# Hybrid attention layer on eight cores: order of the first loads, third projection without shift, kv block of group B ahead of attention A

## The reference

```python
sh1, sc1, ga1, sh2, sc2, ga2 = split(silu(cond) @ w_mod + b_mod, 6)   # cond per request
h = rms_norm(x, g_attn_pre) * (1 + sc1) + sh1
qA, kA, vA, qB, kB, vB = split(h @ w_in)          # w_in: 2048 x 4608
oA = neighbourhood_attention(qA, kA, vA, cache_a_k, cache_a_v, rpb)   # latent: 8 x 16 window plus bias
oB = attend(rope(rms_norm(qB)), [cache_b_k, rope(rms_norm(kB))], [cache_b_v, vB])
x = x + ga1 * rms_norm(concat(oA, oB) @ w_out)
x = x + ga2 * rms_norm(conv_ffn(rms_norm(x) * (1 + sc2) + sh2))
```

## Time and profile before

| what | us |
|---|---|
| median of 3 runs | 3124.49 (3123.12 to 3428.13) |
| the profiled execution, its time | 3145.39 |
| its span on the slowest core (core 2) | 3143.8 |
| spans of its eight cores | 3110.4 to 3143.8 |
| TensorE busy in the span | 2931.7 (93%) |

### The profile page before, as it was taken

The page is one execution under the profiler, slowest core; times in us unless marked ns, Lnnn a source line. Parts: engine busy times, 40 slices in busy tenths (PEclk is TensorE's granted clock), DMA queues, the critical chain, the costliest instruction groups (busy, mean ns, idle before and its releaser), DMA issues.

```text
span 3143.8 us, 39804 instructions; the slowest of 8 cores (3110.4 to 3143.8 us)
## 1 busy us (share of the span) xinstructions
PE 2931.7 (93%) x15020; PEld 1375.2 (44%) x15020; DVE 1304.8 (42%) x1822; ACT 1026.7 (33%) x1787; POOL 157.5 (5%) x263
## 2 busy tenths in 40 slices
PE   0689899989999999999998998989999999999997
PEld 0335433444444444444444444544444444444443
DVE  0326734655540443443444345245540343442445
ACT  1236766444322220220225145644322220220223
POOL 0003500000000000000000000000000000000001
PEclk9999999999999999999998899999999999999999
DMA  9879545594636446438446675383625424435438
GB/s 180 173 128 152 85 78 98 98 195 134 114 66 113 76 72 114 71 64 142 70 83 165 117 153 102 84 170 140 136 54 97 82 51 91 81 62 96 78 64 117
DMA packets 40305, 333.62 MB, mean 106 GB/s; under 512 B 4726, under 2 KB 7846, under 8 KB 15542
## 3 DMA queue, kind: packets, MB, share of 16 engines
q0 software_dynamic: 23472, 263.48, 49.1%
q1 hardware_dynamic: 16646, 67.60, 6.4%
HBM read 533.68 MB, written 44.07 MB: 184 GB/s over the span
## 4 chain that ended last, share of the span: by engine, by line
PE 86%; DMA 5%; ACT 3%; DVE 2%; issue 2%; another core or an unknown queue 1%; POOL 0%; SPq 0%; DVEq 0%; ACTq 0%; POOLq 0%
PE PS L1433 84%; PE PS L1434 2%; ACT M L1435 2%; DMA M<-xs 1%; DMA M<-modrows 1%; ACT M L1436 1%; DMA M<-w_mod 1%; DMA M<-w_in 1%; DMA sbk<-M 1%; DMA M<-xp 0%; DVE M L1441 0%; DVE M L1440 0%; DVE M L1438 0%; ACT stats L1435 0%
## 5 line engine op out<-in xcount | busy, mean ns | idle before, releaser
L1433 PE MATMUL PS<-M 128*128 128x512 bf16 (+2 forms) x12960 | 2812.3, 375 | 37.2 <-ACT M L1435 18.0
L1433 PEld LDWEIGHTS PS<-M 128*128 128x128 bf16 x12960 | 1246.6, 99 | 1508.0 <-issue 197.9
L1441 DVE SCALAR_TENSOR_TENSOR M<-PS,taps,M 128x1023 f32<-128x1023 f32 (+1 forms) x352 | 451.0, 1281 | 784.2 <-ACT M L1435 765.5
L1435 ACT ACTIVATE M<-PS,taps 128x1024 f32<-128x1024 f32 x176 | 211.5, 1203 | 929.5 <-PE PS L1433 929.5
L1435 ACT ACTIVATE M<-M 128x1024 f32<-128x1024 f32 (+5 forms) x268 | 235.7, 879 | 475.4 <-DVE M L1441 297.5
L1439 DVE TENSOR_TENSOR M<-PS,M 128x512 f32<-128x512 f32 (+2 forms) x320 | 204.5, 661 | 401.5 <-PE PS L1433 276.2
L1436 ACT COPY M<-PS 128x512 f32<-128x512 f32 (+5 forms) x309 | 201.7, 664 | 391.0 <-PE PS L1433 302.0
L1434 PE MATMUL PS<-identb,M 128*128 128x128 bf16 x1300 | 114.9, 234 | 114.2 <-DVE M L1440 81.6
L1434 PEld LDWEIGHTS PS<-identb,M 128*128 128x128 bf16 x1300 | 94.1, 105 | 157.0 <-issue 136.0
L1440 DVE TENSOR_SCALAR M<-M,stats 128x256 bf16<-128x256 bf16 (+4 forms) x164 | 89.1, 561 | 157.7 <-ACT stats L1435 143.6
L1435 ACT ACTIVATE M<-PS,negB 128x512 bf16<-128x512 f32 x192 | 128.0, 686 | 44.9 <-PE PS L1433 42.0
(11 more groups left out here) (65 smaller groups left out, 559.6 us busy)
## 6 DMA issues: line engine op xcount, KB each, us to landing
M<-w_up POOLq DMA_DIRECT2D x40, 2048.0 KB, 15.8
M<-w_mod POOLq DMA_DIRECT2D x24, 2048.0 KB, 20.3
M<-w_down POOLq DMA_DIRECT2D x32, 1408.0 KB, 12.1
M<-w_in POOLq DMA_DIRECT2D x18, 2048.0 KB, 17.3
M<-xs SPq DMA_DIRECT2D x16, 1024.0 KB, 17.2
M<-w_out POOLq DMA_DIRECT2D x8, 2048.0 KB, 23.4
M<-xp SPq DMA_DIRECT2D x16, 1024.0 KB, 7.1
ys<-M SPq DMA_DIRECT2D x8, 1024.0 KB, 5.9
```

What stands on the lines that cost most here:

```text
L1433: "matmul": lambda e, kw: e.matmul(**kw),
L1435: "activation": lambda e, kw: e.activation(**kw),
L1441: "scalar_tensor_tensor": lambda e, kw: e.scalar_tensor_tensor(**kw),
```

## The change

1. All eight tiles of latent rows get buffers of their own (`X0`) and their loads are issued right after `cond`; `mrows` goes between the second and the third, and `gq_bc` and `gk_bc` now stand behind all eight on SP's queue. The first weight load waits until the tile with index 5 has landed.
2. The list `FIRST` is reordered: vA0 is loaded right after kA0, ahead of the four `c0` blocks. kvB no longer needs the token, which is gone; `tables` is queued for tick 6.
3. vA0 runs on the scaled, unshifted rows `hS` too: tiles 6 and 7 are copied to SBUF, six tiles stay in PSUM banks 0 to 5. `mod_col(0, 0)` and `(0, 1)` stand between its tiles. The shift's share is a row: 16 matmuls of the broadcast shift `shB` with the weights, added by `fix_v` to each tile. kA0 runs without a `mod_col` in it.
4. `modulate` now gives DVE tokens 0 to 639 and ACT 640 to 1023.
5. kvB of the first group runs alone, before the cached keys and the mask are handled and before attention A starts; attention A is woven into qB0 and qB1 alone, with shares 0.45 and 0.75. The four blocks of `w_mod` that were in kvB and qB0 move on by one projection.

```diff
-                dma("pool", mb(e[3], e[2][0] * e[2][1]), e[1], "w%d" % int(e[3]))
+                dma("pool", mb(e[3], e[2][0] * e[2][1]), e[1], "w%d" % int(e[3]), rk=[("xin", 5)] if i == 0 else ())
...
-        MODS = {"qA0": [], "kA0": [], "vA0": [], "kvB": [(2, 0), (2, 1), (2, 2)], "qB0": [(2, 3)], "qB1": [(3, 0)],
-                "kA1": [(3, 1), (3, 2)], "vA1": [(3, 3), (4, 0), (4, 1)], "qA1": [(4, 2), (4, 3)]}
+        MODS = {"qA0": [], "kA0": [], "vA0": [], "kvB": [], "qB0": [(2, 0), (2, 1)], "qB1": [(2, 2), (2, 3)],
+                "kA1": [(3, 0), (3, 1)], "vA1": [(3, 2), (3, 3), (4, 0)], "qA1": [(4, 1), (4, 2), (4, 3)]}
-        FIRST = [("c", 1, 0, s0), ("qA0", s1), ("c", 1, 1, s2), ("c", 1, 2, WX_AT), ("c", 1, 3, E_AT), ("kA0", s0), ("c", 0, 0, s2), ("c", 0, 1, WX_AT),
-                 ("c", 0, 2, E_AT), ("c", 0, 3, s2), ("vA0", WX_AT), ("kvB", s2), (2, 0), (2, 1), ("qB0", s0), (2, 2), ("qB1", s2), (2, 3),
-                 ("kA1", s0), (3, 0), ("vA1", s2), (3, 1), (3, 2), ("qA1", s0), (3, 3), (4, 0), (4, 1), (4, 2), (4, 3)]
+        FIRST = [("c", 1, 0, s0), ("qA0", s1), ("c", 1, 1, s2), ("c", 1, 2, WX_AT), ("c", 1, 3, E_AT), ("kA0", s0), ("vA0", s2), ("c", 0, 0, WX_AT),
+                 ("c", 0, 1, E_AT), ("c", 0, 2, WX_AT), ("c", 0, 3, E_AT), ("kvB", WX_AT), ("qB0", s0), (2, 0), ("qB1", s2), (2, 1), (2, 2),
+                 ("kA1", s0), (2, 3), (3, 0), (3, 1), ("vA1", s2), (3, 2), (3, 3), ("qA1", s0), (4, 0), (4, 1), (4, 2), (4, 3)]
-                        add_in(g, e[0], e[1], ("S",) if e[0] == "kvB" else ())
+                        add_in(g, e[0], e[1])
...
+        X0 = (32, 40, 48, 56, 144, 152, 172, 180)
+        for t in range(NT):
+            dma("sp", mf(X0[t], 2048), xg[GROUPS[0]][t * 128:(t + 1) * 128, :], "x%d" % t, wk=[("xin", t)])
+            if t == 1:
+                dma("sp", cst[0:48, :], mrows, "ca")
+        dma("pool", maskb[:], mask_d, "c6")
+        w_pump()
         for i, (g_d, g_t) in enumerate(((g_qn, gq_bc), (g_kn, gk_bc))):
             dma("sp", g_t[:], bass.AP(g_d, 0, [[0, 128], [1, 128]]), "c%d" % (2 + i))
...
-            if i in (1, 4):
-                mod_col(0, i // 3, 6, 7)
+        Wv = w_get("in%dvA0" % g)
+        vf = {6: mf(188, 512), 7: mf(190, 512)}
+        vbank = {6: 0, 7: 1, 0: 2, 1: 3, 2: 4, 3: 5, 4: 0, 5: 1}
+        for n, t in enumerate((6, 7, 0, 1, 2, 3, 4, 5)):
+            for c in range(16):
+                mm(bank(vbank[t]), hS[:, c, t * 128:(t + 1) * 128], Wv[:, c, :], c == 0, c == 15)
+            if t > 5:
+                op("act", "copy", out=vf[t], in_=bank(vbank[t]))
+            if n in (1, 5):
+                mod_col(0, n // 4, 6, 7)
         mod_col(0, 2, 6, 7)
         mod_col(0, 3, 6, 7)
+        shB = mb(40, 2048).rearrange("p (c m) -> p c m", c=16)
+        vrow = mf(44, 512)
+        op("dve", "tensor_copy", out=shB, in_=modcols[:, 1, g, :].unsqueeze(2).to_broadcast([128, 16, 128]))
...
+        for c in range(16):
+            mm(bank(6), shB[:, c, :], Wv[:, c, :], c == 0, c == 15)
+        w_done("in%dvA0" % g)
-        modulate(g, 0, 0, 512)
-        modulate(g, 0, 512, 1024, "act")
+        modulate(g, 0, 0, 640)
+        modulate(g, 0, 640, 1024, "act")
+        op("act", "copy", out=vrow, in_=bank(6))
...
+        def fix_v(ts):
+            for t in ts:
+                op("dve", "tensor_tensor", out=vv[:, 2 + t, :, :].rearrange("p h d -> p (h d)"), in0=vf[t] if t > 5 else bank(vbank[t]), in1=vrow, op=ALU.add)
+        fix_v((4, 5, 0, 1, 2, 3))
+        later(3, fix(*fixes[0]))
+        later(4, lambda _: fix_v((6, 7)))
+        later(5, fix(*fixes[1]))
...
-            mark("S")
-        later(4, tables)
+        later(6, tables)
...
+                run_all(dense_in(g, "kvB", (6, 7), (0, 1)))
+                flush((0, 1))
+...
-            for k, nm in enumerate(("kvB", "qB0", "qB1")):
-                corun(dense_in(g, nm, (6, 7), None, mods[nm]), 28.5, sA, (0.28, 0.38, 0.6)[k])
+            for k, nm in enumerate(("qB0", "qB1") if first else ("kvB", "qB0", "qB1")):
+                corun(dense_in(g, nm, (6, 7), None, mods[nm]), 28.5, sA, ((0.45, 0.75) if first else (0.28, 0.38, 0.6))[k])
```

More of the change, by code:

```diff
@@ L402, in build_program @@
                     elif isinstance(e[0], str):
-                        add_in(g, e[0], e[1], ("S",) if e[0] == "kvB" else ())
+                        add_in(g, e[0], e[1])
                     else:
-                        add_mod(*e, WX_AT if e == (2, 1) else s1)
+                        add_mod(*e, s1)
                 homes = (s2, s1, s0, WX_AT)
@@ L423, in build_program @@
                         add_mod(5, M5[qd, j])
-        dma("pool", maskb[:], mask_d, "c6")
-        w_pump()
+        X0 = (32, 40, 48, 56, 144, 152, 172, 180)
+        cst = mf(198, 128)
         dma("sp", identf[:], ident_d, "c0")
@@ L438, in build_program @@
             op("pe", "transpose", out=PS[:, r * 16:(r + 1) * 16], in_=stg0[0:16, r, :], identity=identf[0:16, 0:16])
-        condT = mf(192, 32)
+        condT = mf(191, 32)
         op("dve", "tensor_copy", out=condT, in_=PS[:, 0:32])
@@ L541, in modulate, with norm1 @@
                     op("act", "activation", out=h, in_=h, func=AF.Identity, scale=sc, bias=sh)
-        def norm1(g, x_ats, xn_ats, tb):
+        def norm1(g, x_ats, xn_ats, tb, ahead=True):
             def load(t):
@@ L548, in norm1 @@
             nx = len(x_ats)
-            for t in range(nx - 1):
+            for t in range(nx - 1 if ahead else 0):
                 load(t)
             for t in range(NT + 2):
-                if t + nx - 1 < NT:
+                if ahead and t + nx - 1 < NT:
                     load(t + nx - 1)
@@ L1034, in build_program @@
         g = GROUPS[0]
-        cst = mf(198, 128)
-        dma("sp", cst[0:48, :], mrows, "ca")
         cols = mf(198.5, 48)
@@ L1043, in build_program @@
         qf = [mf(172 + 4 * h, 1024) for h in range(4)]
-        kf = [mf(at, 1024) for at in (160, 164, 144, 148)]
+        kf = [mf(at, 1024) for at in (156, 160, 144, 148)]
         mcnt = [0]
@@ L1049, in by_groups @@
             mcnt[0] += 1
-            part = mf(188 + 2 * (mcnt[0] % 2), 512)
+            part = mf(192 + 2 * (mcnt[0] % 2), 512)
             for cc in range(4):
@@ L1078, in mod_col @@
                 op("dve", "tensor_tensor", out=dst, in0=dst, in1=bc, op=ALU.add)
-        n1 = Side(norm1(g, (144, 152, 172, 180), (160, 164, 168), [(4, 5), (2, 3)]), 10.0)
+        n1 = Side(norm1(g, X0, (160, 164, 168), [(4, 5), (2, 3)], False), 10.0)
         n1.finish()
@@ L1115, in build_program @@
         for k, nm in enumerate(("kA0", "qA0")):
-            fixes.append((nm, 2 + k) + by_groups(shT, w_get("in%d%s" % (g, nm)), 2 + k))
+            part, rest = by_groups(shT, w_get("in%d%s" % (g, nm)), 6 + k)
+            op("dve", "tensor_copy", out=part, in_=bank(6 + k))
+            fixes.append((nm, rest))
             w_done("in%d%s" % (g, nm))
-        modulate(g, 0, 0, 512)
-        modulate(g, 0, 512, 1024, "act")
+        for c in range(16):
[4 more added lines that the diff above has]
+        op("act", "copy", out=vrow, in_=bank(6))
         def fix(nm, rest):
@@ L1133, in fix @@
             return go
[L1135 to L1138, removed]
+        def fix_v(ts):
[5 more added lines that the diff above has]
+        later(5, fix(*fixes[1]))
+        tst = mf(196, 512).rearrange("p (j q) -> p j q", j=4)
         dma("sp", tst[0:88, 0:3, :], conv_w.rearrange("j (c p) -> c j p", p=128), "c4")
@@ L1158, in build_program @@
                 mod_begin(2, 140, 0)
+                run_all(dense_in(g, "kvB", (6, 7), (0, 1)))
+                flush((0, 1))
+                for j in range(4):
+                    op("pe", "transpose", out=PS[:, 512 + j * 88:512 + (j + 1) * 88], in_=tst[0:88, j, :], identity=identf[0:88, 0:88])
+                op("dve", "tensor_copy", out=taps[:, :, :], in_=PS[:, 512:512 + 352].rearrange("p (j c) -> p j c", j=4))
+                for fn in go_on:
+                    fn()
+                bias_mask()
             else:
                 sF = Side(final(GROUPS[0], G2, f_tiles(), fss), 10.0)
[L1161 to L1176, removed]
+            for k, nm in enumerate(() if first else ("qA0", "kA0", "vA0")):
+                corun(dense_in(g, nm, (4, 5, 6, 7), (0, 1), mods[nm]), 28.5, sF, 1.0 / (3 - k))
             while not first and sF.t < 10.0:
```

## The result

The changed kernel takes 3173.33 us (median of 4, 3171.95 to 3175.95) against 3124.48; the ratio is 1.0159, 95% interval 1.0139 to 1.0179. It is 49 us slower; 3141 was forecast, with a range to 3163.

The account below looks back on a forecast made before the run. TensorE, busy 93% of the span, was taken as the bound outside the start. Attention A ending 15 us later, norm1's 5 us gain included, plus a moved block made +16 on 3124.5, rounded to 3141 us; range 3113 to 3163.

Parts of the forecast that it names:

- Part 1: Start, x rows first: norm1 still waits for gq_bc and gk_bc behind x on SP's queue; gain 5 us.
- the bound of 14: Norm1 at the start: upper limit of the gain, 14 us, if each queued load takes 12.2 us.
- The rule of whole packets: DMA queues at the start: round robin by packets would land both gains near 45 us, giving 3118; chance 0.15.
- Part 2: Weight order from qA0 to kvB: kvB's weights land behind c0_3, so kvB starts at 228.5 instead of 233.3 us.
- Part 3: Loads behind kvB: cached keys and bias table queue behind three blocks; first bias at 281.1, about 21 us idle.
- main case: Whole kernel: bias table landing late holds attention A; 3141 us, own range 3131 to 3152, chance 0.60.
- rival B: Before attention A: tables not behind the weights, start near 263 once kvB is flushed; 3123 us, chance 0.08.
- Part 4: Attention A in two projections: weaving no worse, stretch of 128.9 us ending at 410.0, 15 us later than 395.
- sign of being wrong: Attention A: the prediction is wrong if the two projections woven with it take over 60 us each.
- Rival C: Attention A packed too densely: TensorE waits for the exponent every unit, 20 us more; 3161 us, chance 0.12.
- The blocks behind: Stages behind attention A: order kept, weights have over 20 us for a 15.2 us load; moved block adds 1.0.
- runs tell nothing apart within 2%: Whole kernel: no change within 2% (62 us) can be told; same 0.97, faster 0.01, slower 0.02.

Follow-up runs that it names:

- f_part1: Kernel before with only eight x buffers, x rows loaded ahead of the weights and the two gains behind x: 3102.21 us, ratio 0.9935.
- d_token: Changed kernel with the load of qB0 waiting for tables, so cached keys and bias table precede it in the queue: 3174.5 us against 3173.
- c_shares: Changed kernel with attention A's shares in qB0 and qB1 at 0.28 and 0.38 instead of 0.45 and 0.75: 3141.85 us, ratio 1.0063.
- b_kv_woven: Changed kernel with kvB woven into attention A again (shares 0.28, 0.38, 0.6) and qB0's load waiting for tables: 3136.09 us, ratio 1.0043.
- j_mods: Changed kernel with two blocks of w_mod in qA1 instead of three, and three in kA1: 3159.01 us, ratio 1.0117.
- k_cols_early: Changed kernel with the four shift blocks used earlier, two between the tiles of kA0 and two between those of vA0: 3162.75 us, ratio 1.0127.
- e_gains_woven: Changed kernel with the loads of gq_bc and gk_bc ahead of x and kvB woven into attention A again: 3116.77 us, ratio 0.9971.
- m_best_woven: Changed kernel with gains ahead of x, kvB woven into attention A, shift blocks used early and two w_mod blocks in qA1: 3115.85 us, ratio 0.9978.
- h_gains_shares: Changed kernel with the loads of gq_bc and gk_bc ahead of x and shares 0.28 and 0.38: 3119.96 us, ratio 0.9998.
- n_best_alone: Changed kernel with gains ahead of x, shift blocks early, two w_mod blocks in qA1, kvB alone, shares 0.28 and 0.38: 3112.65 us, ratio 0.9969.

## Why the prediction was wrong

**Part 1.** The mechanism held: SP's queue served in order, norm1 behind `gq_bc` and `gk_bc`. The size was off: three turns beside weights were counted, for tile 7 and the two gains, and two came. All of x had been moved by about 30 us (8.5 MB on SP's queue), before the weights took their share, so tile 7 cost no turn; the gains were seen at 45.8 and 59.3, 13.5 us apart instead of 15.5. The gain was 20 us, not 5, and outside the bound of 14. The experiments show it a real gain (f_part1), which the rest gave back. The rule of whole packets in the Trainium skill ("DMA: Bandwidth & Descriptors", "Queues, rings and completion order"), by which, as the prediction worked it out, both gains would land close behind each other, does not fit 45.8 and 59.3.

**Part 2.** The wait for `c0_3` came as worked out (5.9 us), and kvB started at 221.5 instead of 228.5. Against the kernel before, norm1's 20 us were 15 after the stages of qA0, which took 41.3 us instead of 36.6 at a lower granted clock (0.50 to 0.83 in most windows of 10 us between 70 and 120), and 12 at kvB. That the queue stood still for 30 us was in the forecast's own numbers, `c0_2` only after 183, but was not named as a cost.

**Part 3.** The time was right, 281.1 against 279.0 (276.3 by the mean over the cores), but in part by luck, as another wait held it. d_token shows that the loads did not decide: with `rpbt` there 16 us earlier the bias is first added at the same time. What ended last was kvB's flush and, behind it, the chain of the cached keys. The main case had no flush after kvB's matmuls; only rival B had one, at 263.

**Part 4 is the step that failed.** "It fits, tightly" compared busy sums: 44 and 45 us of VectorE and ScalarE beside 54 of TensorE. The stretch was put at 128.9 us and measured 162 (279 to 441). The busy sums were right: qB0 had 41 us of VectorE and 42 of ScalarE, qB1 47 and 45. That they would then run beside TensorE at full rate was wrong: two projections took 79 and 65 us, 144 instead of 108, over the 60 that the prediction had named as a sign of being wrong. The wait that it had left out is TensorE's for the exponent, 2.1 to 2.6 us in about every second unit of qB0's first half and 24 us in all, against 7 in c_shares; most of the rest is matmuls at the lower clock. Rival C had the place and the kind of wait right (TensorE on the exponent), but priced it from the drain at 0.7 us a unit, 20 us in all; its price had to hold the convoy, in which the exponent stands behind a copy that itself waits for TensorE, and the lower clock seen after most of these stops. c_shares takes 31 us back by the shares alone, and its stretch is 129.1 us by the mean over the cores: the time forecast for the weaving is there once attention A is woven in no denser than before. b_kv_woven takes 37 back.

**The blocks behind.** "Over 20 us for a load of 15.2" was worked out for halves. qA1 got three blocks; one was used at 616.0 and the next was wanted 12 us later, so its load was 3.9 us late (632.21 above). The stretch up to the end of qA1 cost 7 us instead of 1, and j_mods takes 6 of them back.

The sum: 15 was forecast for kA1's start. The two traced cores give 46, but the one of before asks for the second cached keys as the first of its eight, at 393.9, and the one of the change as the last, at 438.3; by the means over the cores it is 37 (396.3 and 433.0). That is the 15, less 5 for a first bias ahead of its forecast, and 28 for part 4. For the blocks 1 was forecast and 7 came. Together 44 against the 49 measured on the slowest cores; the other 5 are within what cores differ. By steps between kernels: part 1 -20 (3102), parts 2 to 4 of the change with the new blocks +34 (3136), kvB alone with the higher shares +37 (3173). The prediction's remark that runs tell nothing apart within 2% does not hold for these: the interval of the result is 0.2% to either side.

What stays open is how much of the +34 belongs to vA0 without shift as such: k_cols_early and j_mods give 11 and at least 6 on the changed kernel, but together only 1 on e_gains_woven (m_best_woven) and 7 on h_gains_shares (n_best_alone), and the issue of `tables` behind the fixes was seen in a trace but not tried alone.

## What to carry to other kernels

Busy sums of engines say whether two streams can be woven, not at what rate: if each step of one stream waits, on an engine that runs in order, behind a step of the other, count the chain of one round, in the order in which each engine gets its operations, and try two shares before anything is rebuilt. Moving a projection out of the woven stretch saved nothing here (157 us before and after) until the shares were lowered as well (129). When a consumer of weight blocks is moved later, follow the homes: the block after it can be asked for only then, and the queue may stand still in a place where nobody waits. And small loads that an engine needs first belong ahead of large ones in the same queue; what that is worth depends on what waits next: 20 us in the changed kernel, 5 in the one with part 1 alone. Last, compare stages by the mean over the cores where one execution's cores differ by 12 us, and not by one core of each kernel.

## What was unexpected

The price of a short stop of TensorE: after 2.3 us without a matmul at 301 us, nine matmuls of one kind took 3.68 us instead of 2.00, and windows of 5 us around such stops (300, 310, 320 and 335) had a granted clock of 0.66 to 0.72. In the kernel before, a wait of 2.07 us at 366 left the clock of its window at 1.00. What separates the two was not tested.
